# First modulation rows of a two-block transformer kernel: scale pieces, then x, then shift pieces, the shift summed in columns

## What is computed

```python
mod = (jax.nn.silu(c) @ ada_w[l] + ada_b[l]).reshape(bsz, 6, dm)
shift_a, scale_a, gate_a = mod[:, 0, None, :], mod[:, 1, None, :], mod[:, 2, None, :]
h = rms_norm(x, norm1_g[l]) * (1.0 + scale_a) + shift_a
proj = h @ w_in[l]
```

## Time and profile before

| | us |
|---|---|
| median of the runs | 2497.85 |
| lowest and highest run | 2495.33, 2503.66 |
| the profiled execution, its own time | 2499.09 |
| span of the profiled execution | 2497.5 |
| PE busy in the span | 2400.2 (96%) |
| DVE busy | 1915.3 (77%) |
| ACT busy | 1354.0 (54%) |

### The profile page before, as it was taken

How to read it: one execution, slowest core, us unless ns; L and a number is a source line. 1 busy time by engine, 2 the same in 40 slices (tenths; PEclk the granted TensorE clock), 3 DMA queues, 4 the chain that set the end, 5 groups by cost and what they waited for, 6 DMA issues and landing times. The chain is left out here.

```text
span 2497.5 us, 33891 instructions
## 1 busy us (share of the span) xinstructions
PE 2400.2 (96%) x11969; PEld 1979.8 (79%) x11969; DVE 1915.3 (77%) x2471; ACT 1354.0 (54%) x1924; POOL 590.3 (24%) x492
## 2 busy tenths in 40 slices
PE   7999999899999999999989999999999999999999
PEld 4766678678888887886688999997788888878887
DVE  4876668678989989897877888887766666657786
ACT  3243323357777777775676676776434444444332
POOL 2000444143333233332711111110042333400000
PEclk8999999999999999999999999999999999999999
DMA  6778255589878899998521111113332443587864
GB/s 253 237 246 297 102 208 206 227 318 397 336 270 308 307 398 395 411 394 337 193 69 51 52 52 51 52 39 116 129 110 86 152 167 139 188 314 260 304 252 152
DMA packets 181316, 535.36 MB, mean 214 GB/s; under 512 B 17711, under 2 KB 77715, under 8 KB 167881
## 3 DMA queue, kind: packets, MB, share of 16 engines
q1 hardware_dynamic: 147260, 462.82, 50.6%
q0 software_dynamic: 12592, 45.63, 4.8%
q10 hardware_dynamic: 21340, 25.29, 2.9%
HBM read 443.38 MB, written 90.33 MB: 214 GB/s over the span
## 5 line engine op out<-in xcount | busy, mean ns | idle before, releaser
L1766 PE MATMUL psum<-w_high,block_hT_high 128*128 128x512 f32 x576 | 232.5, 404 | 6.9 <-DVE w_low L1384 5.7
L1384 DVE TENSOR_TENSOR w_low<-first_w_up,w_high 128x2048 fp32r<-128x2048 f32 x72 | 186.5, 2628 | 53.1 <-ACT w_high L1378 53.1
L1768 PE MATMUL psum<-w_high,block_hT_low 128*128 128x512 f32 x576 | 225.3, 391 | 0.0
L1767 PE MATMUL psum<-w_low,block_hT_high 128*128 128x512 f32 x576 | 224.8, 390 | 0.0
L1766 PE MATMUL psum<-w_qkv_high,fox_hT_high 128*128 128x384 f32 (+1 forms) x512 | 181.6, 355 | 8.5 <-DVE w_qkv_low L2613 3.4
L1384 DVE TENSOR_TENSOR w_low<-first_w_gate,w_high 128x2048 fp32r<-128x2048 f32 x74 | 168.6, 2282 | 19.6 <-ACT w_high L1378 19.4
L1766 PE MATMUL psum<-w_mlp_out_high,hidden_part_high 128*128 128x512 f32 x448 | 174.5, 390 | 3.3 <-DVE hidden L4011 1.8
L1480 POOL TENSOR_TENSOR block_out<-block_out,late_rows 128x1024 f32<-128x1024 f32 x35 | 92.7, 2648 | 359.6 <-ACT block_out L1644 359.6
L1378 ACT ACTIVATE w_high<-first_w_gate 128x2048 fp32r<-128x2048 f32 x74 | 141.2, 1912 | 65.4 <-DMA first_w_gate<-in_w_expert_gate 61.6
L1767 PE MATMUL psum<-w_mlp_out_low,hidden_part_high 128*128 128x512 f32 x448 | 174.3, 389 | 0.0
L1768 PE MATMUL psum<-w_mlp_out_high,hidden_part_low 128*128 128x512 f32 x448 | 174.3, 389 | 0.0
(11 more groups left out here) (524 smaller groups left out, 6732.3 us busy)
## 6 DMA issues: line engine op xcount, KB each, us to landing
first_w_gate<-in_w_expert_gate SPq DMA_DIRECT2D x32, 2048.0 KB, 10.0
first_w_up<-in_w_expert_up SPq DMA_DIRECT2D x32, 2048.0 KB, 10.4
first_w_down<-in_w_expert_down SPq DMA_DIRECT2D x31, 2048.0 KB, 10.5
w_mlp_out_quarters<-in_w_mlp_out SPq DMA_DIRECT2D x78, 512.0 KB, 7.0
hidden_part<-hidden_parts SPq DMA_DIRECT2D x54, 512.0 KB, 4.4
v_aug<-in_w_ada SPq DMA_DIRECT2D x48, 512.0 KB, 5.1
expert_rows<-block_out POOLq DMA_DIRECT2D x34, 512.0 KB, 8.3
v_aug<-in_ada_w SPq DMA_DIRECT2D x32, 512.0 KB, 4.8
```

Of the source, the lines that this page charges most:

```text
L1384: dve.tensor_tensor(wl[:, par, half], raw[kind][:, half], wh[:, par, half].bitcast(F32), ALU.subtract).then_inc(s_wl, 1)
L1766: pe.matmul(out, sh, mh, start=start, stop=False)
L1767: pe.matmul(out, sh, ml, start=False, stop=False)
L1768: return pe.matmul(out, sl, mh, start=False, stop=stop)
```

## The change

The shift and the scale are loaded and summed apart. SP issues eight scale pieces (512 KB each, one slot each), norm1_g, x tiles 0 to 3, then eight shift pieces (512 KB each, into the same slots, each behind the use of its scale piece), then w0, x tile 4, w1, x tiles 5 and 6, three later pieces, x tile 7. DVE accumulates scale pieces alone, makes the gain, and then accumulates shift pieces between `scaled(0)`, `scaled(1)` and `scaled(2)`; `hrow` has three buffers.

PE sums the scale as before, turns tiles 0 and 1 without the shift, and then sums the shift as columns: for each odd shift piece eight matmuls with 128 columns of the piece (every eighth) as the stationary operand and one column of silu(c) as the moving one, with `keep_busy` between; at the end eight more with `acc` and a column of ones. DVE copies the 128x8 result twice into `shift_cols`, PE turns it by one transpose, ACT and DVE split it as before, and PE adds the shift to tiles 0 and 1, each with its own signal. ACT's copy of the shift row and PE's sixteen one-row records (L1094) are gone. On DVE `scaled(3)` comes ahead of `h_low(0)`, and `low(0)` behind it.

```diff
-first_rows = yT[:].rearrange("p (r two) n -> p r (two n)", two=2)
+first_rows = yT
 xr = sgo
-hrow, gain, shift = ucT[:, 0:2, :], ucT[:, 2, :], zrow[0:1, 1, :]
-ones_at = sbuf(ctx, "shift_selector", [1, 32 + 2 * KT])
+hrow, gain = [ucT[:, 0, :], ucT[:, 1, :], zrow[:, 1, :]], ucT[:, 2, :]
+shift_cols = sbuf(ctx, "mix_shift_cols", [P, 2, 32])
 shift_parts = sbuf(ctx, "mix_shift_parts", [32 + KT, P], F32R)
-shift_sums = bank[0][0:32 + KT, 0:P]
-s_sel, s_ct, s_ch, s_cl = [sem("m_shift_" + n) for n in ("selector", "turned", "high", "low")]
+shift_sums, shift_turned = bank[0][:, 0:KT], bank[1][0:32 + KT, 0:P]
+s_zc, s_cc, s_ct, s_ch, s_cl = [sem("m_shift_" + n) for n in ("zeroed", "columns", "turned", "high", "low")]
...
-        def first_piece(k):
-            if k >= 4:
-                sp.wait_ge(s_fp if k % 2 else s_f0, k // 2 - 1)
-            sp.dma_start(first_rows[:, k % 4, :], ada[0][:, k, 0:2 * D]).then_inc(s_fr[k % 4], 16)
+        def scale_piece(k):
+            sp.dma_start(first_rows[:, k, :], ada[0][:, k, D:2 * D]).then_inc(s_fr[k], 16)
+
+        def shift_piece(k):
+            if k == KT - 1:
+                sp.wait_ge(s_b0, 1)
+            else:
+                sp.wait_ge(s_fp if k % 2 else s_f0, k // 2 + 1)
+            sp.dma_start(first_rows[:, k, :], ada[0][:, k, 0:D]).then_inc(s_fr[k], 16)
...
                 if b < 2:
-                    sp.wait_ge(s_f0, 1)
+                    sp.wait_ge(s_f0, KT // 2 + 1)
...
         for l, c in enumerate((a["c"], a["c_2"])):
             sp.dma_start(ccol[:, l, :], c[0].rearrange("(p k) -> p k", k=KT)).then_inc(s_c, 16)
-        for k in range(4):
-            first_piece(k)
+        for k in range(KT):
+            scale_piece(k)
             if k == 0:
                 sp.wait_ge(z, 1)
                 for g in range(2):
                     sp.dma_start(bt[0:1, g, :], ada_bias[0][:, g * D:(g + 1) * D]).then_inc(s_mb[g], 16)
         sp.dma_start(spare[:, 3, :], a["norm1_g"].to_broadcast([P, D])).then_inc(s_gr, 16)
-        for k in range(4, KT):
-            first_piece(k)
         for t in range(4):
             x_tile(t)
-            if t == 1:
-                weights(0)
+        for k in range(KT):
+            shift_piece(k)
+        weights(0)
+        x_tile(4)
         weights(1)
+        x_tile(5)
+        x_tile(6)
         for j in range(3):
             piece(j)
-        for t in range(4, TT):
-            x_tile(t)
+        x_tile(7)
...
-        for t in range(3):
+        for t in range(4):
             square(t)
-        act.wait_ge(s_b0, 1)
-        act.wait_ge(z, 2)
-        act.activation(shift, psum[0:1, 0:2, :].rearrange("p b n -> p (b n)"), ACT.Copy).then_inc(s_shift, 1)
-        square(3)
+        act.wait_ge(s_ct, 1)
+        act.activation(shift_parts[:], shift_turned, ACT.Copy).then_inc(s_ch, 1)
         high(0)
-        act.wait_ge(s_ct, 1)
-        act.activation(shift_parts[:], shift_sums, ACT.Copy).then_inc(s_ch, 1)
...
         def scaled(t):
             dve.wait_ge(s_rs, t + 1)
-            if t >= 2:
-                dve.wait_ge(s_tr, t - 1)
-            dve.scalar_tensor_tensor(hrow[:, t % 2, :], xr[:, t % 4, :], stat[:, t, 1:2], gain, ALU.mult, ALU.mult).then_inc(s_sc, 1)
...
-        both = acc[:].rearrange("p q n -> p (q n)")
+        def first_acc(q, n):
+            k = 2 * n
+            dve.wait_ge(s_fr[k], 16 * (2 - q))
+            if n == 0:
+                dve.wait_ge(s_mb[q], 16)
+            else:
+                dve.wait_ge(s_f0, KT // 2 * (1 - q) + n)
+            dve.scalar_tensor_tensor(acc[:, q, :], first_rows[:, k, :], csil[:, 0, k:k + 1], acc[:, q, :] if n else bt[:, q, :], ALU.mult, ALU.add).then_inc(s_f0, 1)
+
...
-        for k in range(0, KT, 2):
-            dve.wait_ge(s_fr[k % 4], 16 * (k // 4 + 1))
-            if k == 0:
-                dve.wait_ge(s_mb[0], 16)
-                dve.wait_ge(s_mb[1], 16)
-            else:
-                dve.wait_ge(s_f0, k // 2)
-            dve.scalar_tensor_tensor(both, first_rows[:, k % 4, :], csil[:, 0, k:k + 1],
-                                     bt[:].rearrange("p q n -> p (q n)") if k == 0 else both, ALU.mult, ALU.add).then_inc(s_f0, 1)
+        for n in range(KT // 2):
+            first_acc(1, n)
...
-        dve.wait_ge(s_b0, 2)
+        dve.wait_ge(s_b0, 1)
...
         dve.wait_ge(s_gain, 1)
         scaled(0)
+        first_acc(0, 0)
         scaled(1)
-        low(0)
+        first_acc(0, 1)
+        dve.wait_ge(z, 2)
+        scaled(2)
+        first_acc(0, 2)
+        first_acc(0, 3)
+        dve.wait_ge(s_zc, 1)
+        dve.wait_ge(s_shift, 1)
+        dve.tensor_copy(shift_cols[:, :, 0:KT], shift_sums.unsqueeze(1).to_broadcast([P, 2, KT])).then_inc(s_cc, 1)
         dve.wait_ge(s_ch, 1)
-        dve.tensor_tensor(shift_parts[32:32 + KT, :], bank[0][32:32 + KT, 0:P], shift_parts[32:32 + KT, :].bitcast(F32), ALU.subtract).then_inc(s_cl, 1)
-        scaled(2)
+        dve.tensor_tensor(shift_parts[32:32 + KT, :], bank[1][32:32 + KT, 0:P], shift_parts[32:32 + KT, :].bitcast(F32), ALU.subtract).then_inc(s_cl, 1)
+        scaled(3)
         for t in range(TT):
             h_low(t)
-            if t + 3 < TT:
+            if t == 0:
+                low(0)
+            if t >= 1 and t + 3 < TT:
                 scaled(t + 3)
             if t == 3:
...
-        def turn(t):
-            if t == 1:
-                pe.wait_ge(pc, 2)
-            if t >= 2:
-                pe.wait_ge(s_hl, t - 1)
-            if t >= 1:
-                shifts(t, True)
+        def turn_rows(t, start):
             pe.wait_ge(s_sc, t + 1)
             for k in range(KT):
-                ins = pe.matmul(turned(t)[:, k, :], hrow[:, t % 2, k:D:KT], ident[:], start=t == 0 and k % 4 == 0, stop=t > 0 and k % 4 == 3, is_transpose=True)
-            if t == 0:
-                pe.wait_ge(s_cl, 1)
-                ins = shifts(t, False)
-            ins.then_inc(s_tr, 1)
+                ins = pe.matmul(turned(t)[:, k, :], hrow[t % 3][:, k:D:KT], ident[:], start=start and k % 4 == 0, stop=not start and k % 4 == 3, is_transpose=True)
+            return ins
+
+        def turn(t):
+            pe.wait_ge(s_hl, t - 1)
+            shifts(t, True)
+            turn_rows(t, False).then_inc(s_tr, 1)
...
         for k in range(1, KT, 2):
             pe.wait_ge(s_cb, k // 2 + 1)
-            pe.wait_ge(s_fr[k % 4], 16 * (k // 4 + 1))
+            pe.wait_ge(s_fr[k], 16)
             if k == KT - 1:
                 pe.wait_ge(s_f0, KT // 2)
-                for q in range(2):
-                    for hf in range(2):
-                        pe.matmul(bank[2 * q + hf], ones[:], acc[:, q, hf * HALF:(hf + 1) * HALF], start=False, stop=False)
-            for q in range(2):
                 for hf in range(2):
-                    at = q * D + hf * HALF
-                    ins = pe.matmul(bank[2 * q + hf], qk[:, k // 2, :], first_rows[:, k % 4, at:at + HALF], start=k == 1, stop=k == KT - 1)
-                if k == KT - 1:
-                    ins.then_inc(s_b0, 1)
-            if k < KT - 1:
-                ins.then_inc(s_fp, 1)
-        keep_busy(pe, bank[6], ident, 2)
-        pe.wait_ge(s_sel, 3)
-        pe.wait_ge(s_shift, 1)
-        for k in range(KT):
-            ins = pe.matmul(shift_sums, ones_at[:, KT - 1 - k:31 + 2 * KT - k], shift[:, k:D:KT], start=k == 0, stop=k == KT - 1)
-        ins.then_inc(s_ct, 1)
-        keep_busy(pe, bank[6], ident, 1)
-        turn(0)
-        turn(1)
-        keep_busy(pe, bank[1], ident, 1)
+                    pe.matmul(bank[2 + hf], ones[:], acc[:, 1, hf * HALF:(hf + 1) * HALF], start=False, stop=False)
+            for hf in range(2):
+                ins = pe.matmul(bank[2 + hf], qk[:, k // 2, :], first_rows[:, k, hf * HALF:(hf + 1) * HALF], start=k == 1, stop=k == KT - 1)
+            ins.then_inc(s_b0 if k == KT - 1 else s_fp, 1)
+        keep_busy(pe, bank[1], ident, 2)
+        turn_rows(0, True)
+        pe.wait_ge(pc, 2)
+        turn_rows(1, True)
+        for k in range(1, KT, 2):
+            pe.wait_ge(s_fr[k], 32)
+            for j in range(KT):
+                pe.matmul(shift_sums[:, j:j + 1], first_rows[:, k, j:D:KT], csil[:, 0, k:k + 1], start=k == 1 and j == 0, stop=False)
+            keep_busy(pe, bank[1], ident, 2 if k < KT - 1 else 1)
+        pe.wait_ge(s_f0, KT)
+        for j in range(KT):
+            ins = pe.matmul(shift_sums[:, j:j + 1], acc[:, 0, j:D:KT], ones[:, 0:1], start=False, stop=j == KT - 1)
+        ins.then_inc(s_shift, 1)
+        pe.wait_ge(s_cc, 1)
+        pe.transpose(shift_turned, shift_cols[:].rearrange("p r k -> p (r k)")[:, 0:32 + KT], ident[:]).then_inc(s_ct, 1)
+        pe.wait_ge(s_cl, 1)
+        for t in range(2):
+            shifts(t, False).then_inc(s_tr, 1)
         turn(2)
         turn(3)
         turn(4)
```

(11 more changed lines are left out.)

## The result

The changed kernel takes 2509.96 us (median of nine runs, 2507.16 to 2522.28) against 2497.85 for the kernel before: 1.0058 of its time, 95% interval 1.0042 to 1.0074, so 10 to 18 us slower. A second set of the same kernel gave 1.0073 (1.0045 to 1.0101). The forecast was 2502, with 0.74 on "same". The time is within 0.32% of it and inside the range of 2491 to 2512, but no change was forecast, and the kernel is slower by more than the interval allows for chance.

A forecast was written before the change was run, and what follows sets the result against it. PE, busy 96% of the span, was taken as the bound, so only the first input product's start counted: 59.9 against 55.73, +4.2 on 2499.09, 2503.3, or 2502 against the median. Range 2491 to 2512.

The forecast's parts named there:

- same: Whole program: time within about 0.3% (7.5 us) of the kernel before, chance 0.74.
- the price of a column product: Shift sum on PE: sixteen one-column records take 1.87 us at full clock (0.117 each), 3.8 at the low clock.
- the return of the clock after the first group: Shift sum: first group and its keep_busy at 1.2 GHz until 35.7, then full clock, sums ready at 47.5.
- What bounds the kernel: Whole kernel: PE is busy 96% of the span, so early changes only move when it starts working without a break.
- the mark: Start of the first input product on PE, taken to move the end: 59.9 against 55.73, +4.2 us.
- Loads, scale and gain: Start of kernel: gain ends at 20.7, 15 us ahead; shift piece 0 lands at 24.0, last piece at 33.4.
- The sentence on the bounds: Price of sixteen one-column records in the shift sum: not over 1.87 us at full clock, at least a third of that.
- Rival C: Shift sum: clock does not recover because half of each round is one-column products; slower once over two groups run low; chance 0.27.
- full form: Rival C with all five groups at the low clock: first product at 72.7, +17, time 2515; chance 0.15.
- rule of transposes: PE clock in the shift sum: transposes do not count as busy for the clock, which gives Rival C its chance.
- estimate of 1.7 a group: Shift sum: sixteen weight loads at 107 ns take 1.7 us at either clock; first group 2.1 shorter, time 2500; not adopted.
- Sums to first product: After the shift sum: small steps 1.4 us, tile 0 signalled 0.7 later, then eight DVE steps, 10.3, to 59.9.

The follow-up runs named there:

- first execution: The changed kernel as first profiled, nothing altered: 2508.33 us, first input product at 72.69 us.
- second execution: The changed kernel traced once more, nothing altered: first input product at 73.52 us, ratio of its set 1.0073 against the kernel before.
- column form: Changed kernel without keep_busy between column-product groups; fills in waits (three between turning tiles 0 and 1, two behind their shift products) added: ratio 1.0019, first product 60.17.
- row form: Changed kernel's new loads, but shift summed by 512-column products and row copy as before: ratio 1.0015, first product 58.03; with fills in waits 1.0, 57.50.

## Why the prediction was wrong

Two steps failed: the price of a column product, put at 0.117 us a record at full clock, and the return of the clock after the first group. Together they are 10.7 of the 12.8 us by which the forecast start of the first product, 59.9, missed 72.69.

**What bounds the kernel.** Right as far as it shows: a late first product comes out in the program's time, with a scatter of some us that the text did not allow for. Of 17 us at the mark 9.2 and 16.0 reached the end of the two traced executions.

**Loads, scale and gain.** Right to 0.7 us: gain 20.06 to 21.28 (forecast end 20.7), shift piece 0 waited for until 24.46 (24.0), tile 1 turned at 27.09 (26.6), at the low clock as forecast, first group at 28.82 (28.5).

**The price of a column product.** This is the first step that failed. It took the router's 36-column products (0.117 a record) as the nearest row and gave the low clock alone the 0.24. The operands of those products are contiguous, those of the new ones take every eighth float. Measured: 0.23 to 0.25 at either clock. Counted from start to start the five groups took 18.2 us instead of 11.3, 6.9 of the 12.8 us by which 59.9 missed 72.69. The sentence on the bounds said "not over 1.87 at full clock"; the stride made it 3.7, above what was given as the upper bound. The strided rows in the trace, the turning of tiles (1.16 for 8 records at the high clock), could have warned only a little: they are 0.145 a record, against 0.117.

The 0.24 at the low clock came from a doubtful reading that gave about the right number. The loads of 337 ns were put down to the low clock, but all of them start by 33.3, where the earlier trace rows has a granted clock of 1.00. Those at 11.56, 12.41, 13.27 and 14.12 start 0.86 us apart, which is the pace of the low clock, so the granted clock in the rows is no proof of the pace there. Loads at a granted 0.50 bear the price out: the fills' loads at 33.46 and 34.31 in the changed kernel take 0.34 us.

**The clock.** This is the second. Forecast: one group and one block at 1.2 GHz, then 2.4 for good. Shown: in the first execution the clock did come back at 35.3, near the end of the first block, then fell at 38.7 during the next group. The same came twice more (up at 42.1 and 48.9, down at 45.5 and 52.4), so that the blocks ran almost wholly at 1.2 GHz and the high stretches fell on products that do not profit from them. In the second execution it never came back. The blocks took 11.5 us instead of 7.7, 3.8 of the miss. Rival C named this mechanism and its outcome (first product 72.7, measured 72.69), with 0.15 for the full form; its place was right, but half of its reason, slow groups because of the clock, was wrong: with the clock up they are as slow. That the two numbers agree so closely is luck: C had the sums ready 1.0 us later than measured (59.5 against 58.5) and the way from there 1.0 shorter. The fall at 25.0 tests no rule of transposes, since PE had turned one tile since 21.7 and stood idle for the rest.

The rule that C took from the Trainium skill (TensorE: Matmul & The Clock Gate, Part 4) is that transposes do not count as busy. The trace agrees in the tile loop of the changed kernel, where PE is busy with transposes and shift products from 63.81 to 72.69 and stays at 0.50. The rule alone does not account for the kernel before, whose clock held at 1.00 from 48.7 to 55.5 in the same loop. The Trainium skill (the same page, section on LDWEIGHTS) prices a load by its columns, which gives an estimate of 1.7 a group: 1.84 contiguous comes near it at the high clock; 3.41 at the low clock and 3.73 strided do not.

**Sums to first product.** The four small steps took 1.36 (forecast 1.4). The tile loop was forecast at 10.3 from the first tile's signal; it took 11.55 at the low clock, where PE with 3.05 us a tile sets the pace instead of DVE: 1.2, and the shift products before it 0.6 over. The rest (0.3) is the later start. 6.9 + 3.8 + 1.2 + 0.6 + 0.3 = 12.8.

**Where luck helped.** The time missed by 8 us where the mark missed by 12.8, because not all of the delay reached the end. It lies inside the range although the range left the full rival C out, at 2515, and the first product came where full C had it.

**What the forecast left aside.** The kernel before has one `keep_busy` ahead of tile 2, and its clock rose at 48.7; the change drops it. What that block alone is worth was not tried. Two blocks there won 0.6 us of the tile loop in the column form and lost 1.8 in the row form.

## What to carry to other kernels

Price a product by a row of the same kind with the same access pattern of its stationary operand, not only the same shape: here the stride alone doubled a product, and no clock helped. Filler matmuls between groups on the path cost their full time, at the low clock double, and are worth it only if what follows gets faster with the clock. Where the engine waits they are cheaper, but only as long as they end with the wait; here none of the kernels that had them there was shown to be faster than the kernel before. When a path is made of small instructions, forecast both clock levels for its whole length and give the lower one real weight.

## What was not expected of the hardware

- fp32 products with a 128x128 stationary operand that takes every eighth float: 0.23 to 0.25 us a record at a granted clock of 1.00 and of 0.50 (3.73 to 3.96 for 16). Contiguous: 0.115 to 0.122 (1.84 and 1.95) at 1.00 and 0.21 to 0.22 (3.41 and 3.57) at 0.50. One or 64 moving columns made no difference. Transposes with the same stride do not pay it: their loads take 185 to 226 ns, against 312 to 339.
- One or two fills ahead of the tile loop did not bring its clock back reliably: with them it stayed at 0.50 to the first product in four kernels (57.78, 57.50, 53.44, 54.31) and came back at 47.2 and 53.4 us in two (54.03, 60.17).
- A DVE accumulation whose output is written with a stride of 128 floats takes 1.99 to 2.01 us instead of 1.28.
- The same program's clock between 28 and 70 us differs between two executions (1.00 in three stretches, or never).
